# Zero rows for a short tile: one shape for every product of a one-hot gather

## The reference, cut to what matters

```python
def _trunk(x, ...):
    x = x + mix                                   # mixer, 304 x 1024
    x = x + _hier_moe(_rmsnorm(x, norm2_g[l]), ...)
    return _rmsnorm(x, final_norm_g), ...

def _hier_moe(xn, ...):
    gidx = top_k(xf @ w_group + b_group, 1)       # one group of 4
    eidx = top_k(el_sel, 2)                       # two experts of its 8
    for e in range(N_EXPERTS):
        he = silu(xf @ w_exp_gate[e]) * (xf @ w_exp_up[e])
        y = y + combine[:, e:e + 1] * (he @ w_exp_down[e])
```

## Time and profile before

| what | value |
|---|---|
| profiled execution | 724.03 us |
| its span, first to last instruction | 722.2 us |
| TensorE products busy | 639.4 us (89%) |
| TensorE weight loads busy | 479.1 us (66%) |
| VectorE busy | 546.0 us (76%) |
| ScalarE busy | 374.7 us (52%) |
| GpSimd busy | 135.7 us (19%) |
| moved by DMA | 160.29 MB |
| mean granted clock of TensorE | 0.938 |

### The profile page before, as it was taken

One profiled execution on the slowest core, in us unless ns is written; L12 is line 12 of the kernel. 1 busy time (PEld: TensorE's weight loads), 2 busy tenths in 40 slices (PEclk: granted clock), 3 DMA queues, 4 the chain that ended last, 5 costly groups with the idle time before them and its releaser, 6 DMA issues.

```text
span 722.2 us, 8206 instructions
## 1 busy us (share of the span) xinstructions
PE 639.4 (89%) x2972; PEld 479.1 (66%) x2972; DVE 546.0 (76%) x753; ACT 374.7 (52%) x524; POOL 135.7 (19%) x102
## 2 busy tenths in 40 slices
PE   6999999894784969999999899999999999999910
PEld 5677777672784959997786566666666666666600
DVE  2079987899899999864368588888788877888406
ACT  2120113551921514754256487887788888888412
POOL 1019861252493610040000000000000000000030
PEclk9799999998797989999989999999999999999975
DMA  9766063333033332504080699999999999997143
GB/s 270 224 189 233 1 233 117 116 117 116 2 116 117 117 116 99 167 8 169 1 348 1 253 342 388 404 393 412 388 420 393 402 396 404 408 399 272 44 162 119
DMA packets 46070, 160.29 MB, mean 222 GB/s; under 512 B 7574, under 2 KB 10886, under 8 KB 33718
## 3 DMA queue, kind: packets, MB, share of 16 engines
q1 hardware_dynamic: 39232, 154.13, 56.4%
q10 hardware_dynamic: 6086, 3.06, 1.9%
q0 software_dynamic: 704, 2.49, 1.0%
HBM read 145.51 MB, written 15.02 MB: 222 GB/s over the span
## 4 chain that ended last, share of the span: by engine, by line
PE 55%; DVE 4%; ACT 2%; issue 2%; DMA 1%; POOL 0%; POOLq 0%; DVEq 0%; ACTq 0%
PE bank L1601 25%; PE bank L1626 14%; PE bank L1420 7%; PE bank L1515 5%; PE bank L1564 2%; DMA ring<-expert_rows,row_i 1%; ACT hi_gu L805 1%; PE bank L1613 1%; PE bank L1487 1%; DVE x L1337 1%; DVE conv L1067 1%; DVE gel_lo L1025 0%; PE bank L1477 0%; DVE x L1351 0%; POOL ring L542 0%
## 5 line engine op out<-in xcount | busy, mean ns | idle before, releaser
L1259 DVE TENSOR_TENSOR lo_gu<-ring,hi_gu 128x2048 fp32r<-128x2048 f32 x64 | 143.8, 2288 | 37.2 <-ACT hi_gu L805 37.2
L1425 PE MATMUL bank<-work,ring 128*128 128x304 f32 x512 | 134.6, 423 | 0.9 <-ACT work L589 0.9
L957 DVE SCALAR_TENSOR_TENSOR work<-work,par 128x272 f32<-128x272 f32 x240 | 131.6, 619 | 0.0
L1425 PEld LDWEIGHTS bank<-work,ring 128*128 128x128 f32 x512 | 98.2, 192 | 35.3 <-issue 2.2
L805 ACT ACTIVATE hi_gu<-ring 128x2048 fp32r<-128x2048 f32 x64 | 118.5, 1900 | 0.0
L1601 PE MATMUL bank<-hi_gu,xe_hi 128*96 128x512 f32 x256 | 103.0, 402 | 2.1 <-issue 2.1
L1601 PE MATMUL bank<-lo_gu,xe_hi 128*96 128x512 f32 x256 | 101.0, 395 | 0.0
L1601 PE MATMUL bank<-hi_gu,xe_lo 128*96 128x512 f32 x256 | 100.7, 393 | 0.0
L542 POOL DMA_INDIRECT ring<-expert_rows,row_i x6 | 5.7, 954 | 329.6 <-DMA expert_rows<-outst 328.0
L1420 PE MATMUL bank<-xn_hi,w_hi 128*128 128x304 f32 x128 | 41.4, 324 | 27.1 <-DVE xn_lo L1025 15.1
L1626 PE MATMUL bank<-ring,windows 128*96 128x512 f32 x128 | 65.3, 592 | 0.0
(11 more groups left out here) (278 smaller groups left out, 1136.2 us busy)
## 6 DMA issues: line engine op xcount, KB each, us to landing
ring<-w_exp_gate SPq DMA_DIRECT2D x32, 1024.0 KB, 7.2
ring<-w_exp_up SPq DMA_DIRECT2D x32, 1024.0 KB, 9.5
ring<-w_exp_down SPq DMA_DIRECT2D x32, 1024.0 KB, 9.5
ring<-w_in SPq DMA_DIRECT2D x11, 2048.0 KB, 8.1
expert_rows<-outst SPq DMA_DIRECT2D x32, 384.0 KB, 7.4
ring<-w_rnn_proj SPq DMA_DIRECT2D x2, 2048.0 KB, 8.0
ring<-w_conv_proj SPq DMA_DIRECT2D x2, 2048.0 KB, 8.5
ring<-w_out SPq DMA_DIRECT2D x2, 2048.0 KB, 8.2
```

The costliest lines, as they stand in the source:

```text
L957: ins = vec.scalar_tensor_tensor(y, glu[:, ch, w:w + TP], pcw[:, w, ch:ch + 1], y, ALU.mult, ALU.add)
L1259: vec.tensor_tensor(part, whole, as_f32(high), ALU.subtract).then_inc(out_done, 1)
L1425: ins = mm(bank[m % 4][:, 0:T], mix_w[b % MIX_SLOTS][:, i, (c % MB) * P:(c % MB + 1) * P], xnT[:, i], start=(i == 0), stop=(i == KT - 1))
```

## The change: what it does

The third token tile gets 128 rows in the gather. The rows 48 to 127 of `halves` are written with zeros by VectorE, two memsets for each part (32 partitions from row 32 on and 64 from row 64 on; rows 32 to 47 are then overwritten with tokens). `sel` is computed for all 128 rows of every tile, and all 96 products read 128 rows. A semaphore `pad_done` orders the zeros before the tokens and before the products; in a second pass the zeros are written anew.

```diff
-            def high_rows(n, t):
+            def high_rows(n, t, r=0):
 
                 m = ROWS[t]
+                if n == 0 and t == NT - 1:
+                    act.wait_ge(pad_done, 2 * r + 1)
                 nc.scalar.activation(halves[0:m, 0, t, :, n * 64:n * 64 + 64], by_channel(x[0:m, t, n * 512:(n + 1) * 512]),
                                      ACT.Copy).then_inc(hi_done, 1)
...
+            def pad(i):
+
+                for p in (32, 64):
+                    ins = vec.memset(as_f32(halves[p:2 * p, i, NT - 1]), 0.0)
+                ins.then_inc(pad_done, 1)
+
             def low_rows(n, t, r=0):
 
                 m = ROWS[t]
+                if n == 0 and t == NT - 1:
+                    dve.wait_ge(pad_done, 2 * r + 2)
                 dve.wait_ge(hi_done, r * (2 * NT) + (n * NT + t + 1))
...
             for t in range(NT):
                 residual(0, t)
+            pad(0)
             dve.wait_ge(router_in, 64)
...
             low_rows(0, 0)
             turned(0)
             turned(2)
             dve.wait_ge(half_mm, 2)
+            pad(1)
             low_rows(0, 1)
             low_rows(0, 2)
...
                 for t in range(NT):
-                    n = ROWS[t]
-                    step(vec.tensor_scalar(sel[0:n, t], iota[0:n], pos2[0:n, t:t + 1], None, ALU.is_equal))
-                    vec.scalar_tensor_tensor(sel[0:n, t], iota[0:n], pos1[0:n, t:t + 1], as_f32(sel[0:n, t]),
+                    step(vec.tensor_scalar(sel[:, t], iota, pos2[:, t:t + 1], None, ALU.is_equal))
+                    vec.scalar_tensor_tensor(sel[:, t], iota, pos1[:, t:t + 1], as_f32(sel[:, t]),
                                              ALU.is_equal, ALU.add).then_inc(sel_done, 1)
...
+                dve.wait_ge(dn_mm, r * NE)
+                pad(0)
+                pad(1)
                 for n, t in itertools.product(range(2), range(NT)):
                     low_rows(n, t, r)
...
                 def gather(q, t):
 
-                    n = ROWS[t]
                     for i in range(2):
-                        ins = mm(bank[q % 4][:, 0:T], halves[0:n, i, t, q // 2], sel[0:n, t, (q % 2) * T:(q % 2 + 1) * T],
+                        ins = mm(bank[q % 4][:, 0:T], halves[:, i, t, q // 2], sel[:, t, (q % 2) * T:(q % 2 + 1) * T],
                                  start=(t == 0 and i == 0), stop=(t == NT - 1 and i == 1))
...
                 pe.wait_ge(lo_done, r * (2 * NT) + 2 * NT)
+                pe.wait_ge(pad_done, 2 * r + 2)
                 for t in range(NT):
```

More of the change, by code:

```diff
@@ L239, in trunk @@
          st_cp, st_T, st_ev, st_out, mean_mm, cen_done, sq_done, sum_done, var_mm, var_done, std_done, nrm_done, silu_done,
-         merged, wo_mm, x1_done, ss2_done, ms2_done, rs2_done, xT2_mm, ss_half, xT2_act, xT2_dve,
+         merged, wo_mm, x1_done, ss2_done, ms2_done, rs2_done, xT2_mm, pad_done, ss_half, xT2_act, xT2_dve,
          log_mm, place_step, mo_done, ex_req, ex_done, pick_done, rank_mm, iota_done, sel_done, gat_mm, gat_done,
@@ L250, in trunk @@
             "st_cp st_T st_ev st_out mean_mm cen_done sq_done sum_done var_mm var_done std_done nrm_done silu_done "
-            "merged wo_mm x1_done ss2_done ms2_done rs2_done xT2_mm ss_half xT2_act xT2_dve "
+            "merged wo_mm x1_done ss2_done ms2_done rs2_done xT2_mm pad_done ss_half xT2_act xT2_dve "
             "log_mm place_step mo_done ex_req ex_done pick_done rank_mm iota_done sel_done gat_mm gat_done "
@@ L860, in again @@
                 for n, t in itertools.product(range(2), range(NT)):
-                    high_rows(n, t)
+                    high_rows(n, t, r)
                 experts(r)
```

## The result

The changed kernel takes **720.06 us**, the median of six runs (719.03 to 721.14). The kernel before took 735.6 us in six runs beside them, but these lie at two levels: 723.51 and 724.29, and 735.2 to 737.47. The ratio of 0.9945 (95% interval 0.9925 to 0.9965) compares the changed kernel with the lower level alone; that is 4.0 us less, 2.5 to 5.4. From median to median it is 15.5 us, or 2.1%. What the upper level is turned out to be the main finding (e9, e13).

What follows compares the result with a forecast made beforehand. The prediction took TensorE's chain as the bound, with 14.80 us of gathers on it slowed by row-count changes. 724.0 us less 4.8 for the gathers, zeros costing 0, gave 719.2 us, range 716 to 731.5.

Steps and rivals of the forecast that it cites:

- The gathers: 72 products on TensorE: equal 128-row shapes remove the pauses, 14.8 to 10.0 us, 4.8 us less (4.2 to 5.1).
- Who follows: Work behind the gathers moves with their end; VectorE's 5.37 us of idleness bounds the gain, 0.6 us of it left.
- The zeros at no cost: Two memset pairs on VectorE, 1.8 us each, covered by 4.2 and 5.6 us of slack: cost 0.
- The rival of slow memsets: Past 4.2 us a pair TensorE stalls at the second transposes; at 9.0 us a pair the gain is spent; chance 0.02.
- The clock behind the gathers: First expert's 1.8 us loss after TensorE's idle stretch stays; rivals: it vanishes (717.4 us, 0.12) or doubles (721.0, 0.08).
- The level: Whole kernel: 719.2 us forecast from the lower-level profiled execution; the change said not to touch the spread's cause.
- "730.4 us" on the level of the median: Whole kernel: the same 4.8 us gain taken on the level of the shown runs' median instead of the profiled execution.
- About 2% as the bound of what can be told: Measurement tells about 2% from no change; gain 0.7%, so within 2% got 0.92, faster 0.05, slower 0.03.
- its own bounds: Whole kernel: the forecast's range with the clock's loss vanishing or doubling, from 717 to 721.8 us.

Runs made afterwards that it cites:

- e9: The kernel before, unchanged, one more profiled execution, which fell on the upper level: 734.96 us.
- e13: The changed kernel with all 96 gathers reading 48 rows, rows 48 to 127 of the full tiles left out: twelve runs at 728.6 to 733.2 us.
- e1: The changed kernel, zeros and waits kept, with the third token tile's gathers reading 48 rows: four runs at 722 to 726 us, six at 734 to 737.
- e2: The changed kernel with the third token tile's gathers reading 64 rows: two runs at 723 to 725 us, two at 736 to 737.
- e3: The changed kernel with the third token tile's gathers reading 96 rows: six runs at 718.5 to 721.2 us, ratio 0.994.
- e8: The changed kernel with each pair of memsets written four times: 731.51 us (ten runs, 730.4 to 733.7).
- e12: The changed kernel plus eight products behind the slot products that only keep TensorE at work while it waits for the first windows: 718.70 us.
- e4: The kernel before, later twelve output tiles taking token tiles in alternate order, leaving 12 row-count changes of 24: 732.26 us, ratio 1.0111.
- e7: The changed kernel, 128-row gathers, without the twelve products ahead of them that only keep TensorE at work: four runs at 717.1 to 722.3 us.
- e6: The changed kernel with 48 rows in the third tile's gathers, without the twelve clock-keeping products ahead: runs at 723, 727, 738 and 741 us.

## Why the prediction was right and where it was wrong

- **The gathers: right.** 10.0 us forecast, 10.35 measured, a gain of 4.45 us between the bounds of 4.2 and 5.1. The pause was of the row count (e1, e2, e3), and the switch is not at any difference.
- **Who follows: right.** VectorE's idleness fell to 0.89 us (0.6 forecast), and windows, loads and experts moved along.
- **The zeros at no cost: right**, by e1 and by the transposes, which moved by no more than was there ahead of the zeros. The pair takes 2.3 us, not 1.8, because of the idleness ahead of each memset. The rival of slow memsets counted one stall; by e8 the second pair's stall adds to the first's, so the gain would have been spent at less than 9.0 us a pair.
- **The clock behind the gathers: it stayed**, with 7.34 us for the first expert. It is worth 1.4 us (e12).
- **The level: wrong, and this is the step that failed.** The text said that "the change touches nothing that the trace names as the cause of that spread", and gave as forecast 719.2 us, a sum on the lower level, beside a time before of 735.2, which is on the upper one: 16.0 us less, of which its own mechanism gives 4.8. Level against level the measured gain is 4.0 us. The spread was the clock in the very products that the change lengthens to 128 rows: 12.0 us in the gathers, the slot products and the first expert (e9). So the change takes the upper level away: no run of a kernel with 96 or 128 rows in the third tile's gathers (31 runs in six kernels; e8's ten runs, slower by their memsets, lie at one level of their own) was there, where the kernel before was in 37 of 60, and "730.4 us" on the level of the median was not seen. That the medians lie 15.5 us apart, near those 16.0, is luck: the prediction had no reason for it, and had ruled out the one that the runs showed. The profile of the lower level could not show it, with a clock of 1.00 through the gathers; but the 72 products at twice the time, an estimate from the forecast's own 10.0 us, would be 10 us longer, nearly the distance of the two levels, and that was a reason to ask.
- **About 2% as the bound of what can be told: wrong.** The changed kernel's six runs lie within 0.3%, the kernel before's lower level within 0.4%, and the interval of the ratio is 0.2% either way, so a change of 0.55% is clear of noise. A slip in the working: the upper of "its own bounds", 721.8 us, is 721.6 by its terms (724.0 - 4.2 + 1.8).

Not settled: why the clock falls in some executions of one kernel and not in others, and why e4, with half the changes, was slow in all four runs (low clock in the one profiled), when the kernel before is at its upper level in 37 of 60. e4 puts four short products in a row and the kernel before two; no run varies that alone. Products of 128 rows with pauses were not tried either, so the pauses' own share in the clock is open.

## What to carry to other kernels

Where products that sum over 48 or 64 rows alternate with longer ones, look for a pause with no releaser ahead of its weight loads; zeros up to 96 or 128 rows remove it, if another engine writes them under cover. Where the runs of a kernel lie at two levels, profile an execution of each before working out a change: the difference may sit in one stretch, and that stretch may be yours. A cover of a few microseconds is worth more than its length, since breaking it can cost the clock too.

## What the runs showed of the hardware

- Changing between 48 or 64 rows and 128 cost 0.185 us a change at full clock (e1, e2); between 96 and 128 nothing (e3). At the low clock the pause in the loads was 0.30 us (e9), and a change cost about 0.255 us (e9 against e4).
- A stretch of back-to-back products with 48 rows ran at clock 0.50 in e13, one with 128 rows at 1.00 in the changed kernel. From 0.50 the clock came back to 1.00 while gathers of 128 rows ran (e7), and in the profile of 48 rows among 128 too (e6); in 18 us of 48 rows alone it did not (e13).
- A memset from partition 32 or 64 on had 0.25 to 0.27 us of idleness ahead of it with nothing that the trace shows to wait for (three of the four in the changed kernel; the fourth waited for TensorE).
